# The group norm of a two-block transformer's first attention: its inverse root as a power on GpSimd

## The chip, the cores and the metric

The kernel runs on one core of a Trainium2 chip. The metric is the device time of one execution in microseconds, as the median of several runs. Engines are called TensorE (PE in the rows), VectorE (DVE), ScalarE (ACT), GpSimd (POOL) and SyncE (SP); PEld is TensorE's load of weights.

## What is computed

Two transformer blocks of depth 1 over 1024 tokens of width 1024, in float32. The first block has an RMS norm, a projection, four differential heads (two softmaxes each, subtracted) and eight heads with forget gates, an output projection and a gated feed-forward part. The second has two causal convolutions, eight heads of stick-breaking attention and a feed-forward part with a squared ReLU. The change touches only the norm of the differential heads' outputs:

```python
def rmsnorm(x, g):
    xf = x.astype(jnp.float32)
    y = xf * lax.rsqrt(jnp.mean(xf * xf, axis=-1, keepdims=True) + EPS)
    return (y * g.astype(jnp.float32)).astype(x.dtype)
...
            p = (jax.nn.softmax(jnp.where(chunk_mask, s1, NEG), axis=-1)
                 - lam * jax.nn.softmax(jnp.where(chunk_mask, s2, NEG), axis=-1))
            od = jnp.einsum('bhqk,bhkd->bhqd', p.astype(dv_t.dtype), dv_t)
...
        od_b = rmsnorm(od_b, subln_g[l]) * (1.0 - lam_init)
```

It is taken over the 128 values of a head, for each of four heads and 1024 tokens, with EPS = 1e-5.

## The kernel before

Activations lie transposed in SBUF: 128 features on the partitions, tokens along the row, in two halves of 512. A float32 product of a weight tile is made of three matmuls of 128x512: weights rounded to a high part (`wh`, written by ScalarE, L2411) and a rest (`lows`, written by GpSimd, L2655), each with the activations' high part (L1801, L1803), and `wh` with their rest (L1806). ScalarE and GpSimd make these parts for each piece of weights ahead of TensorE; there are seven buffers for values and rests and four for high parts.

In the stage around the change, attention of one head and the projection of the next ones are interleaved: between score blocks (L1879, L1880), transposes (L1893) and products with the values (L1911, L1914) TensorE takes pieces of projection. VectorE takes a score block's maximum (`max`, L2077 and L2079), ScalarE its exponential with the sum (L2508), VectorE divides (L2096 to L2104). It also evacuates the projections: `qkv_evac` (L2057, L2059) into a stage buffer, and `rotate` (L2066). GpSimd finishes the rotation (L2661, L2679) and splits q and k (L2692, L2694).

A head's output is gathered in four groups of 256 tokens in `mix`, a single buffer of 128x1024 (`diff_out`, L2142; in the later heads with forget gates `pair_out`, L2148). After the last group the norm follows, in two halves of 512 tokens:

- `sub_square`: ScalarE squares `mix` into a stage buffer `i` (L2534).
- `sub_sum`: TensorE multiplies by a matrix of ones, so that each row of PSUM holds the sum over the head (L1921).
- `sub_norm` on VectorE: `va` = -(mean + EPS) / 2 into a stage buffer `j` (L2155).
- `sub_roots`, once for both halves, on ScalarE: y = exp(-0.5 ln(-2 va)), two logarithms (L2540), then two exponentials (L2544). The compiler puts a table load before each pair.
- `sub_norm` on GpSimd, for each half: y (1.5 + va y y), a Newton step, times the gain, and the product into `mix` (L2701, L2703, L2706, L2708, L2710), each waiting for the one before by a semaphore.

The signal `sub` of the last operation frees both stage buffers of its half and lets SyncE spill `mix` to DRAM (L2816); the next write into `mix` waits for that spill. The first writer after the heads one to three is L2142, after the fourth L2148.

The order of work on each engine is not written by hand. `work_order` lays the steps out; `engine_orders` counts each step with rough costs (`about`), lays all engines' steps out on a time axis (`lay_out`), ranks the steps of all engines but TensorE by how late they may run, and repeats that three times; the best result is each engine's order. So a changed cost or step can move others on every engine.

Of the kernel before, what the change touches and what calls it, by code (L numbers as in the profile page):

```python
# [10 lines left out]
ALU = mybir.AluOpType  # L11
ACT = mybir.ActivationFunctionType
# [52 lines left out]
class Part:  # L65


    def __init__(self, place, step):
        self.place, self.step, self.needs, self.gives, self.takes, self.shared, self.bytes = place, step, [], [], 0.0, 0.0, 0
        self.rank = self.start = self.end = 0.0  # L70


def elements(ap):
    n = 1
    for d in ap.shape[1:]:
        n *= d
    return n


def about(engine, op, a, k):  # L80

    n = elements(a[0])
    if engine == "sync":
        return 350.0
    if engine == "tensor":
        if op == "transpose":
            return 110.0
        n = elements(a[2])
        if a[2].dtype == F:
            return max(4 * n / 2.4, 150.0)  # L90
        return 127.0 if a[2].dtype == BF else max((n + 32) / 2.4, 110.0)
    if engine == "scalar":
        return 205 + 0.833 * n
    if engine == "gpsimd":
        if op == "dma_start":
            return 900.0
        return 150 + (1.2 if op == "tensor_scalar" else 2.4) * n
    if op == "tensor_tensor_reduce":
        return 160 + 1.04 * n
    if op == "reduce_max":  # L100
        return 160 + 1.04 * elements(a[1])
    if op == "tensor_tensor_scan":
        return 160 + 2.08 * n
    if n <= 8:
        return 160.0
    if op == "memset" or op == "tensor_scalar" and in_sbuf(op, a):
        return 120 + 0.52 * n
    return 160 + 1.04 * n


def in_sbuf(op, a):

    return op != "memset" and all("PS" not in str(x) for x in a[:4])


class Uncounted:


# [3 lines left out]
    def __getattr__(self, op):  # L122
        def call(*a, **k):
            if self.sg is not None and op != "wait_ge":
                if self.sg.log is not None and op != "then_inc":
                    self.sg.log.takes += about(self.engine, op, a, k)
                    if self.engine == "vector" and in_sbuf(op, a) and elements(a[0]) > 8:
                        self.sg.log.shared += about(self.engine, op, a, k)
                    if op == "dma_start":
                        self.sg.log.bytes += 4 * 128 * elements(a[0])  # L130
            return self
        return call
# [677 lines left out]
class Attention:  # L810
# [60 lines left out]
    def group_steps(self, g, u, a, c, jobs, slot, last):  # L871
        O = self.O
        pending = None
        first = [True]

        def pv(kp, x, end=False):
            given = []
            if first[0]:
                given = O.claim(self.OB) + u.v
            O.step("pv", u=u, a=a, c=c, g=g, kp=kp, x=x, first=first[0], given=given, ob=self.OB)  # L880
            first[0] = False
            self.pt_given[x] = [("pv", (g, kp))]
            u.pv_done = ("pv", (g, kp))

        for kp in range(c + 1):
            tb, given = O.next_t()
            x = self.turned % 2
            self.turned += 1
            O.step("turn", u=u, g=g, kp=kp, c=c, slot=slot, p=[("p", j["key"]) for j in jobs], tb=tb, given=given, x=x, pt=list(self.pt_given[x]))
            if kp == c:  # L890
                self.p_given[slot] = [("turned", (g, kp))]
            O.bank_given[tb] = [("pt_hi", (g, kp)), ("pt_lo", (g, kp))]
            if pending is not None:
                pv(*pending)
            pending = (kp, x)
            yield
        pv(*pending)
        qc = slice(256 * c, 256 * c + 256)
        done = ("pv", (g, c))
        out = ("mix", (g, "out"))  # L900
        if u.kind == DIFF:
            O.step("diff_out", g=g, c=c, qc=qc, done=done, ob=self.OB, given=list(self.mix_given))
            O.bank_given[self.OB] = [out]
        else:
            i, gi = O.next_stage()
            O.step("pair_out", g=g, a=a, qc=qc, done=done, ob=self.OB, i=i, gi=gi, given=list(self.mix_given))
            O.bank_given[self.OB] = [("pair_lo", g), out]
            O.stage_given[i] = [out]
        if not last:
            return  # L910
        row = u.index + (0 if u.kind == DIFF else 4)
        if u.kind == DIFF:
            yield
            squares, roots = [], []
            for half in range(2):
                i, gi = O.next_stage()
                O.step("sub_square", g=g, half=half, i=i, gi=gi, out=out)
                squares.append(i)
            means = [O.next_stage() for _ in range(2)]
            for half in range(2):  # L920
                i = squares[half]
                yield
                b = self.OB
                O.step("sub_sum", g=g, half=half, i=i, b=b, given=O.claim(b))
                yield
                j, gj = means[half]
                O.step("sub_norm", g=g, half=half, i=i, j=j, gj=gj, b=b)
                roots.append((half, i, j))
                if half:
                    O.step("sub_roots", g=g, roots=roots)  # L930
                O.bank_given[b] = [("sub_mean", (g, half))]
                out = ("sub", (g, half))
                O.stage_given[i] = [out]
                O.stage_given[j] = [out]
                yield
        if self.direct is None:
            O.step("spill_mix", row=row, out=out, key=(self.name, row))
            self.mix_given = [("spilled", (self.name, row))]
            self.spills[row] = ("spilled", (self.name, row))
            return  # L940
        dst, ready, free = self.direct
        self.mix_given = []
        for half in range(2):
            key = (self.name, row, half)
            O.step("mix_split", dst=dst, row=row, half=half, key=key, out=out, given=[free])
            ready[row] += [("row_hi", key), ("row_lo", key)]
            self.mix_given += [("row_hi", key), ("row_lo", key)]
        self.spills[row] = None
# [983 lines left out]
def vector_program(e, w, sg, T, steps):  # L1932
    PS = T.PS
    stage, sm, rstd = T.stage, T.sm, T.rstd
    for s in steps:
        kind = s["kind"]
# [9 lines left out]
        elif kind == "lambda":  # L1946
            w.wait_ge(*sg.at("vec", 0))
            e.tensor_tensor(T.gfa, T.vec[:, V_GF:V_GF + 8], T.vec[:, V_GA:V_GA + 8], ALU.mult).then_inc(*sg.up("gfa", 0))
            e.tensor_tensor(sm[:, 2:4], T.vec[:, V_LAM:V_LAM + 2], T.vec[:, V_LAM + 2:V_LAM + 4], ALU.mult)
            e.tensor_scalar(sm[:, 1:2], T.v(V_SUB), 1.0 - LAM_INIT, None, ALU.mult).then_inc(*sg.up("lam_steps", "in"))  # L1950
        elif kind == "lambda_out":
            w.wait_ge(*sg.at("lam_exp", 0))
# [9 lines left out]
        elif kind == "h_in":  # L1962
            k, half = s["e"], s["half"]
# [12 lines left out]
        elif kind == "end_square" and s["i"] is not None:  # L1976
            k, half = s["e"], s["half"]
# [423 lines left out]
def scalar_program(e, w, sg, T, steps):  # L2401
    PS, stage, sm = T.PS, T.stage, T.sm
    for s in steps:
# [127 lines left out]
        elif kind == "sub_square":  # L2531
            for event in s["gi"] + [s["out"]]:
                w.wait_ge(*sg.at(*event))
            e.activation(stage[s["i"]], T.mix[:, cols(s["half"])], ACT.Square).then_inc(*sg.up("sub_sq", (s["g"], s["half"])))  # L2534
        elif kind == "sub_roots":
            for half, i, j in s["roots"]:
                key = (s["g"], half)
                w.wait_ge(*sg.at("sub_mean", key))
                w.wait_ge(*sg.at("sub_summed", key))
                e.activation(stage[i], stage[j], ACT.Ln, scale=-2.0).then_inc(*sg.up("sub_ln", key))  # L2540
            for half, i, j in s["roots"]:
                key = (s["g"], half)
                w.wait_ge(*sg.at("sub_ln", key))
                e.activation(stage[i], stage[i], ACT.Exp, scale=-0.5).then_inc(*sg.up("sub_root", key))  # L2544
        elif kind == "mix_split" or kind == "row_split":
            half, row = s["half"], s["row"]
            if kind == "mix_split":
# [97 lines left out]
def gpsimd_program(e, w, sg, T, steps):  # L2645
    stage = T.stage
    for s in steps:
# [48 lines left out]
        elif kind == "sub_norm":  # L2696
            key, half = (s["g"], s["half"]), s["half"]
            y, va = stage[s["i"]], stage[s["j"]]
            m = T.mix[:, cols(half)]
            w.wait_ge(*sg.at("sub_root", key))  # L2700
            e.tensor_tensor(va, va, y, ALU.mult).then_inc(*sg.up("sub_part", (key, 0)))  # L2701
            w.wait_ge(*sg.at("sub_part", (key, 0)))
            e.tensor_tensor(va, va, y, ALU.mult).then_inc(*sg.up("sub_part", (key, 1)))  # L2703
# [192 lines left out]
def lay_out(lanes, ahead):  # L2896


    given, free, moved = {}, {engine: 0.0 for engine in lanes}, 0.0
    laid = []  # L2900
    at = {(engine, kind): 0 for engine in lanes for kind in lanes[engine]}
    left = sum(len(parts) for kinds in lanes.values() for parts in kinds.values())
    while left:
# [28 lines left out]
                        start, kind, part = begin, other, urgent  # L2932
        part.start = start
        end = start + part.takes
        if engine == "vector" and free["gpsimd"] > start:
            end += 0.6 * min(part.shared, free["gpsimd"] - start)
        free[engine] = end
# [163 lines left out]
```

## Time and profile before

| | us |
|---|---|
| median of 3 runs | 2393.03 (2392.59 to 2394.03) |
| the profiled execution, its own time | 2393.43 |
| its span, first to last instruction | 2391.6 |
| TensorE's matmuls busy | 2339.2 |
| VectorE, GpSimd, ScalarE busy | 1892.4, 1117.8, 1089.0 |

The span is what the trace covers; the execution's own time holds 1.8 us around it. Busy time of an engine doesn't say that it bounds the kernel: where matmuls are busy all the time, what other engines do is hidden. The granted clock is TensorE's, as a share of 2.4 GHz.

### The profile page before, as it was taken

The page shows a single profiled execution, that of the slowest core. Times are in us where ns is not written, and L with a number is a line of the kernel's source. Part 1 is how long each engine was busy: PE and PEld are TensorE (multiplying, and loading weights), DVE is VectorE, ACT ScalarE, POOL GpSimd, SP SyncE. Part 2 cuts the span into 40 slices and gives each one's busy share as a digit, 9 for nine tenths or more (in the row PEclk, how much of TensorE's full clock was granted, in tenths as well). Part 3 has the DMA queues.
Part 4 walks back from the last instruction along what each step waited for, and adds up shares of the span by engine and source line. Part 5 has one row for each costly group of instructions (what it writes and reads, how often), then busy time and mean ns, then how long its engine had stood idle before and what let it go on. Part 6 is the DMA issues. An engine that isn't in the chain of part 4 may idle for free.

```text
span 2391.6 us, 31516 instructions
## 1 busy us (share of the span) xinstructions
PE 2339.2 (98%) x11126; PEld 1933.7 (81%) x11126; DVE 1892.4 (79%) x2593; ACT 1089.0 (46%) x1867; POOL 1117.8 (47%) x786
## 2 busy tenths in 40 slices
PE   9999999999999999999999999999999999999998
PEld 7777778878788888888887877887878888888886
DVE  6777759784687998899967956778288889999986
ACT  6455556562543333353444436555163333544433
POOL 4766652221534664445543553431154466455553
PEclk9999999999999999999999999999999999999999
DMA  4312321242122333264513862223223444754522
GB/s 159 80 45 58 89 76 58 79 129 77 47 74 84 104 104 111 88 210 123 183 58 116 185 153 63 62 60 106 82 82 113 150 150 164 239 160 151 179 89 106
DMA packets 228763, 265.83 MB, mean 111 GB/s; under 512 B 18296, under 2 KB 139640, under 8 KB 228480
## 3 DMA queue, kind: packets, MB, share of 16 engines
q1 hardware_dynamic: 225008, 251.50, 33.5%
q0 software_dynamic: 3168, 11.54, 2.6%
q8 instruction: 90, 1.47, 0.3%
q10 hardware_dynamic: 432, 0.79, 0.1%
q14 instruction: 65, 0.53, 0.1%
HBM read 173.02 MB, written 60.33 MB: 98 GB/s over the span
## 4 chain that ended last, share of the span: by engine, by line
PE 84%; DVE 6%; POOL 3%; ACT 3%; issue 2%; DMA 1%; SPq 0%; POOLq 0%; DVEq 0%; ACTq 0%
PE PS L1801 24%; PE PS L1806 24%; PE PS L1803 24%; PE PS L1893 3%; PE PS L1914 2%; PE PS L1911 2%; PE PS L1879 2%; PE PS L1880 1%; DVE R L2242 1%; ACT R L2565 1%; POOL stage L2679 0%; DVE X L2173 0%; DVE Pb L2102 0%; DVE X L2290 0%; DVE Pb L2104 0%
## 5 line engine op out<-in xcount | busy, mean ns | idle before, releaser
L1801 PE MATMUL PS<-R,wh 128*128 128x512 f32 x2872 | 1138.7, 396 | 9.9 <-DVE stage L2066 2.8
L1806 PE MATMUL PS<-R,wh 128*128 128x512 f32 x2872 | 1122.3, 391 | 3.6 <-DVE R L2238 2.0
L2655 POOL TENSOR_TENSOR lows<-values,wh 128x512 fp32r<-128x512 f32 (+1 forms) x486 | 689.4, 1423 | 899.2 <-ACT wh L2411 737.3
L1803 PE MATMUL PS<-R,lows 128*128 128x512 f32 x2564 | 1001.4, 391 | 0.5 <-POOL lows L2655 0.5
L1801 PEld LDWEIGHTS PS<-R,wh 128*128 128x128 f32 x2872 | 540.4, 188 | 123.7 <-DVE stage L2066 4.5
L1806 PEld LDWEIGHTS PS<-R,wh 128*128 128x128 f32 x2872 | 539.8, 188 | 122.7 <-DVE R L2238 3.7
L2411 ACT ACTIVATE wh<-values 128x512 fp32r<-128x512 f32 (+2 forms) x487 | 301.9, 620 | 613.1 <-PE PS L1806 608.8
L1803 PEld LDWEIGHTS PS<-R,lows 128*128 128x128 f32 x2564 | 482.8, 188 | 95.6 <-issue 4.1
L2290 DVE TENSOR_TENSOR X<-PS,X 128x1024 f32<-128x1024 f32 x154 | 187.2, 1216 | 23.1 <-PE PS L1806 22.5
L2655 POOL TENSOR_TENSOR late_r<-late,wh 128x512 fp32r<-128x512 f32 x77 | 107.8, 1400 | 125.1 <-DVE values L2187 54.7
L2525 ACT ACTIVATE PT<-PS 128x512 fp32r<-128x512 f32 (+1 forms) x200 | 109.0, 553 | 111.0 <-PE PS L1893 89.1
L1803 PE MATMUL PS<-R,late_r 128*128 128x512 f32 x308 | 119.9, 389 | 0.0
L1879 PE MATMUL PS<-R 128*128 128x512 f32 (+2 forms) x288 | 105.2, 369 | 12.2 <-ACT P L2508 7.2
L1893 PE MATMUL PS<-ident,Pb 128*128 128x128 f32 x720 | 107.3, 273 | 8.4 <-DVE PT L2135 3.1
L2114 DVE TENSOR_TENSOR_SCAN Pb<-TABF,steps 128x128 f32<-128x128 f32 (+3 forms) x64 | 94.6, 1486 | 20.4 <-ACT TABF L2517 12.3
L1893 PEld LDWEIGHTS PS<-ident,Pb 128*128 128x128 f32 x720 | 84.6, 141 | 27.4 <-issue 8.5
L2279 DVE TENSOR_TENSOR R1f<-R1f 128x512 f32<-128x512 f32 x88 | 95.3, 1112 | 13.1 <-ACT R1f L2610 12.2
L2193 DVE TENSOR_TENSOR stage<-PS,stage 128x512 f32<-128x512 f32 x140 | 94.4, 681 | 12.1 <-PE PS L1806 10.4
L1880 PE MATMUL PS<-R 128*128 128x512 f32 (+2 forms) x288 | 97.3, 348 | 0.0
L1911 PE MATMUL PS<-PT,R 128*128 128x256 f32 x480 | 89.6, 282 | 3.4 <-issue 1.8
L2411 ACT ACTIVATE wh<-late 128x512 fp32r<-128x512 f32 x77 | 48.5, 629 | 95.5 <-PE PS L1806 95.5
L2137 DVE TENSOR_TENSOR PT<-PS,PT 128x512 fp32r<-128x512 f32 (+1 forms) x120 | 75.0, 632 | 20.7 <-ACT PT L2525 19.7
(278 smaller groups left out, 2976.5 us busy)
## 6 DMA issues: line engine op xcount, KB each, us to landing
scr_hid<-R1f SPq DMA_DIRECT2D x160, 256.0 KB, 2.7
values<-w_in_dram SPq DMA_DIRECT2D x88, 256.0 KB, 2.9
R1f<-scr_hid SPq DMA_DIRECT2D x88, 256.0 KB, 3.8
R0f<-scr_hid SPq DMA_DIRECT2D x86, 256.0 KB, 3.7
values<-w_ff_dram SPq DMA_DIRECT2D x60, 256.0 KB, 3.0
values<-w_ff_dram SPq DMA_DIRECT2D x100, 128.0 KB, 2.5
R<-R SPq DMA_DIRECT2D x96, 128.0 KB, 2.3
X<-X POOLq DMA_DIRECT2D x22, 512.0 KB, 5.7
```

Of the source, the lines that this page charges most:

```text
L1801: e.matmul(PS[:, b, :], wh, high, start=s["start"], stop=False, skip_group_check=on)
L1803: e.matmul(PS[:, b, :], wl, high, start=False, stop=False, skip_group_check=on)
L1806: m = e.matmul(PS[:, b, :], wh, low, start=False, stop=s["stop"], skip_group_check=on)
L1879: e.matmul(S2[:, k0:k1], q, u.KH[:, a, k0:k1], start=True, stop=False)
L1880: m = e.matmul(S2[:, k0:k1], q, u.KL[:, a, k0:k1], start=False, stop=True)
L1893: m = e.transpose(PS[:, s["tb"], at:at + 128], T.Pb[:, s["slot"], par, 128 * kt:128 * kt + 128], T.ident[:, :])
L1911: e.matmul(o, lhs, T.PT[:, x, 0, kk], start=s["first"] and n == 0, stop=False)
L2279: e.tensor_tensor(T.hid_sum(a), one, other, op).then_inc(*sg.up("block", ("sum", *key)))
L2290: e.tensor_tensor(x, T.PS[:, s["b"]:s["b"] + 2, :], x, ALU.add).then_inc(*sg.up("block", s["key"]))
L2411: e.activation(T.wh[:, piece.h, 0:m], T.wv[piece.v][:, 0:m], ACT.Copy).then_inc(*sg.up("w_hi", piece.n))
L2525: e.activation(T.PT[:, s["x"], 0, 0:m], PS[:, s["tb"], 0:m], ACT.Copy, bias=bias).then_inc(*sg.up("pt_hi", key))
L2655: e.tensor_tensor(T.wl[piece.v][:, 0:m], T.wv[piece.v][:, 0:m], T.wh[:, piece.h, 0:m].bitcast(F), ALU.subtract).then_inc(*sg.up("w_lo", pi ...
```

## The change

`sub_roots` and its four activations per head are gone. In their place GpSimd takes -2 va, and that to the power of -0.5, as an operation on two tensors whose second input is one column, broadcast; the column is written once by VectorE. The Newton step stays. GpSimd now waits for `sub_mean` and no more for `sub_root`.

The planner gets a rule: an activation whose function isn't the one of the last table counts 1283 ns more on ScalarE.

```diff
+TABLES = (ACT.Exp, ACT.Ln, ACT.Sqrt, ACT.Silu, ACT.Sigmoid)
+TABLE_LOAD = 1283.0
...
+                    if op == "activation" and a[2] in TABLES:
+                        self.sg.log.tables.append(a[2])
...
-                roots.append((half, i, j))
-                if half:
-                    O.step("sub_roots", g=g, roots=roots)
...
+            e.memset(sm[:, 116:117], -0.5)
...
-        elif kind == "sub_roots":
-            for half, i, j in s["roots"]:
-                key = (s["g"], half)
-                w.wait_ge(*sg.at("sub_mean", key))
-                w.wait_ge(*sg.at("sub_summed", key))
-                e.activation(stage[i], stage[j], ACT.Ln, scale=-2.0).then_inc(*sg.up("sub_ln", key))
-            for half, i, j in s["roots"]:
-                key = (s["g"], half)
-                w.wait_ge(*sg.at("sub_ln", key))
-                e.activation(stage[i], stage[i], ACT.Exp, scale=-0.5).then_inc(*sg.up("sub_root", key))
...
-            w.wait_ge(*sg.at("sub_root", key))
+            w.wait_ge(*sg.at("sub_mean", key))
+            e.tensor_scalar(y, va, -2.0, None, ALU.mult).then_inc(*sg.up("sub_part", (key, "mean")))
+            w.wait_ge(*sg.at("sub_part", (key, "mean")))
+            w.wait_ge(*sg.at("lam_steps", "in"))
+            e.tensor_tensor(y, y, T.sm[:, 116:117].broadcast_to([128, 512]), ALU.pow).then_inc(*sg.up("sub_part", (key, "root")))
+            w.wait_ge(*sg.at("sub_part", (key, "root")))
             e.tensor_tensor(va, va, y, ALU.mult).then_inc(*sg.up("sub_part", (key, 0)))
...
+        for function in part.tables:
+            if function != table:
+                table, end = function, end + TABLE_LOAD
```

In the changed file the lines of TensorE, VectorE and ScalarE have numbers higher by five (L2066 is L2071 there, L2137 is L2142, L2142 is L2147, L2411 is L2416, L2508 is L2513), those of GpSimd ahead of the norm lower by five (L2655 is L2650); the new operations are L2696 and L2699, and L2701 to L2710 keep their numbers.

ScalarE at the norm of the first head, before. `mix` is the head's output, `stage` the buffers:

```order
L2534 ACTIVATE stage<-mix 128x512 [waits s_mix]
L2534 ACTIVATE stage<-mix 128x512 [waits s_qk_lo,s_qk_hi]
L2508 ACTIVATE P_61,sm<-PS,sm 128x384 [waits s_max,s_p]
L2411 ACTIVATE wh<-values 128x512 [waits s_dense,s_raw6]
L2508 ACTIVATE Pb,sm<-PS,sm 128x512 [waits s_max]
L2540 ACT_TABLE_LOAD [waits s_sub_summed]
L2540 ACTIVATE stage<-stage 128x512 [waits s_sub_mean]
L2540 ACTIVATE stage<-stage 128x512 [waits s_sub_summed,s_sub_mean]
L2544 ACT_TABLE_LOAD
L2544 ACTIVATE stage<-stage 128x512 [waits s_sub_ln] x2
L2411 ACTIVATE wh<-values 128x512 [waits s_dense,s_raw0]
L2508 ACTIVATE P_61,sm<-PS,sm 128x512 [waits s_max,s_p]
```

And with the change:

```order
L2539 ACTIVATE stage<-mix 128x512 [waits s_mix]
L2539 ACTIVATE stage<-mix 128x512 [waits s_qk_lo,s_qk_hi]
L2530 ACTIVATE PT<-PS 128x384 [waits s_pv,s_turned]
L2416 ACTIVATE wh<-values 128x512 [waits s_dense,s_raw6]
L2513 ACTIVATE Pb,sm<-PS,sm 128x512 [waits s_max]
L2416 ACTIVATE wh<-values 128x512 [waits s_dense,s_raw0]
L2513 ACTIVATE P_61,sm<-PS,sm 128x512 [waits s_max,s_p]
```

The loads, logarithms and exponentials are gone, the weight split follows the score block's exponential at once, and one exponential (L2508 before, L2513 now) has moved ahead of the squares.

GpSimd at the same place, with the change. The first row is the weight split's neighbour, a rotation; the last two follow the norm's second half:

```order
L2656 TENSOR_TENSOR stage<-stage,TABF 128x512 [waits s_permuted]
L2696 TENSOR_SCALAR stage<-stage 128x512 [waits s_sub_mean]
L2699 TENSOR_TENSOR stage<-stage,sm 128x512 [waits s_lam_steps,s_sub_part]
L2701 TENSOR_TENSOR stage<-stage 128x512 [waits s_sub_part]
L2703 TENSOR_TENSOR stage<-stage 128x512 [waits s_sub_part]
...
L2710 TENSOR_TENSOR mix<-mix,stage 128x512 [waits s_sub_part]
L2674 TENSOR_TENSOR stage<-stage 128x512 [waits s_rot_sin,s_rot_cos]
L2650 TENSOR_TENSOR lows<-values,wh 128x512 [waits s_w_hi]
```

Two operations stand ahead of the five of each half; a rotation and a weight split stand behind the norm, as before.

VectorE behind the norm, before:

```order
L2104 TENSOR_SCALAR Pb<-Pb,sm 128x640 [waits s_inverse]
L2137 TENSOR_TENSOR PT<-PS,PT 128x512 [waits s_pt_hi]
L2077 MEMSET PS 64x64 [waits s_scores]
L2079 TENSOR_REDUCE sm<-PS 128x1 [waits s_masked]
L2066 TENSOR_TENSOR stage<-PS,TABF 128x512 [waits s_permuted,s_sub]
L2096 RECIPROCAL sm<-sm 128x1 [waits s_exp]
```

And with the change:

```order
L2082 MEMSET PS 64x64 [waits s_scores]
L2084 TENSOR_REDUCE sm<-PS 128x1 [waits s_masked]
L2071 TENSOR_TENSOR stage<-PS,TABF 128x512 [waits s_permuted,s_sub]
L2082 MEMSET PS 64x64 [waits s_scores]
L2084 TENSOR_REDUCE sm<-PS 128x1 [waits s_masked]
L2142 TENSOR_TENSOR PT<-PS,PT 128x512 [waits s_pt_hi]
```

The rotation that waits for the norm's first half (`s_sub`) now stands ahead of one more maximum and of the evacuation of a transpose. TensorE's own order differs in exchanges of neighbouring steps up to about 600 us and around the second attention, and is the same in the feed-forward stages; apart from the norm every engine issues the same matmuls, activations and transfers; one table load of the second attention (L2637) is gone too.

## Rows read from the trace of the kernel before

**Rows 1.** The page: span, busy time, chain that ended last.

```profile
span 2391.6 us, 31516 instructions
...
PE 2339.2 (98%) x11126; PEld 1933.7 (81%) x11126; DVE 1892.4 (79%) x2593; ACT 1089.0 (46%) x1867; POOL 1117.8 (47%) x786
...
PE 84%; DVE 6%; POOL 3%; ACT 3%; issue 2%; DMA 1%; SPq 0%; POOLq 0%; DVEq 0%; ACTq 0%
```

**Rows 2.** Table by stretches: busy time by engine, granted clock, DMA share, GB/s.

```profile
0.00:350.00 350.00, 329.43 (x1647) 265.11 (x1648) 253.59 (x492) 191.60 (x350) 211.78 (x161) 1.00 0.29 84
...
2350.00:2391.60 41.60, 32.22 (x158) 27.01 (x156) 27.21 (x48) 13.70 (x23) 11.46 (x9) 0.86 0.33 120
```

**Rows 3.** Waits of TensorE, 120 to 350 us: total, times, longest.

```profile
PE PS L1879 <- ACT P L2508: 6.2, 3, 2.5
...
PE PS L1801 <- DVE late L2059: 1.4, 1, 1.4
```

**Rows 4.** Timeline, first head's norm: start, us, instructions, [idle before].

```profile
136.15 1.28 ACT L2540 ACT_TABLE_LOAD   x1
...
139.91 1.15 ACT L2544 ACTIVATE stage<-stage 128x512 f32<-128x512 f32 x2
...
142.39 0.47 PE L1879 MATMUL PS<-R 128*128 128x512 f32 x1 [2.51 <-ACT P L2508]
```

**Rows 5.** Chain of work by time, first and fourth head: start, us.

```profile
140.62 1.27 POOL stage L2701
...
174.15 1.73 POOL lows L2655
...
335.07 1.30 POOL late L2701
...
346.70 1.29 POOL mix L2710
```

**Rows 6.** Groups of ScalarE's instructions: busy us, mean ns, idle before.

```profile
L2540 ACT ACT_TABLE_LOAD x4 | 5.1, 1283 | 0.1
```

**Rows 7.** Groups of GpSimd's instructions at the norm.

```profile
L2701 POOL TENSOR_TENSOR stage<-stage 128x512 f32<-128x512 f32 x6 | 8.6, 1427 | 9.9 <-ACT stage L2544 9.9
...
L2706 POOL TENSOR_SCALAR stage<-stage,sm 128x512 f32<-128x512 f32 x7 | 5.7, 815 | 0.7
...
L2701 POOL TENSOR_TENSOR late<-late,stage 128x512 f32<-128x512 f32 x1 | 1.3, 1288 | 1.8 <-ACT stage L2544 1.8
```

**Rows 8.** Timeline of GpSimd, first and second head.

```profile
140.62 1.27 POOL L2701 TENSOR_TENSOR stage<-stage 128x512 f32<-128x512 f32 x1 [4.60 <-ACT stage L2544]
141.97 1.27 POOL L2703 TENSOR_TENSOR stage<-stage 128x512 f32<-128x512 f32 x1
...
204.82 1.29 POOL L2701 TENSOR_TENSOR stage<-stage 128x512 f32<-128x512 f32 x1 [2.41 <-ACT stage L2544]
...
214.17 0.69 POOL L2706 TENSOR_SCALAR stage<-stage,sm 128x512 f32<-128x512 f32 x1
...
216.32 1.42 POOL L2710 TENSOR_TENSOR mix<-mix,stage 128x512 f32<-128x512 f32 x1
```

**Rows 9.** Timeline of VectorE: first, second, third and fourth head.

```profile
136.00 0.69 DVE L2155 TENSOR_SCALAR stage<-PS 128x512 f32<-128x512 f32 x1 [0.67 <-PE PS L1921]
...
219.91 0.68 DVE L2057 SCALAR_TENSOR_TENSOR stage<-PS,rstd 128x512 f32<-128x512 f32 x1
...
289.83 0.42 DVE L2142 COPY mix<-PS 128x256 f32<-128x256 f32 x1
...
348.02 0.69 DVE L2059 TENSOR_TENSOR late<-PS,rstd 128x512 f32<-128x512 f32 x1 [1.89 <-POOL mix L2710]
...
352.40 0.42 DVE L2148 TENSOR_TENSOR mix<-PS,stage 64x256 f32<-64x256 f32 x1 [2.64 <-DMA scr_mix<-mix]
```

**Rows 10.** SyncE's spill of mix: third head's issue, landing of all.

```profile
285.04 0.33 SPq L2816 DMA_DIRECT2D scr_mix<-mix  x1
...
DMA to landing us min/median/max: 2.6/2.6/4.5
```

More of the change, by code:

```diff
@@ L70, in __init__ @@
         self.rank = self.start = self.end = 0.0
+        self.tables = []
 def elements(ap):
@@ L913, in group_steps @@
             yield
-            squares, roots = [], []
+            squares = []
             for half in range(2):
@@ L2899, in lay_out @@
     given, free, moved = {}, {engine: 0.0 for engine in lanes}, 0.0
-    laid = []
+    laid, table = [], None
     at = {(engine, kind): 0 for engine in lanes for kind in lanes[engine]}
```

## The prediction

> **What bounds the kernel now.** The page comes first: TensorE's matmuls are busy for 98% of the span, and of the chain of work that ended last 84% is TensorE, 3% GpSimd and 3% ScalarE [rows 1]. So an edit counts where TensorE stands idle, or where it makes it so. The table by stretches says where: in the first 350 us, the stage in which the first attention's four differential heads run, matmuls are busy for 329.4 us and idle for 20.6, of 52.4 in the whole span [rows 1, 2]. The waits of TensorE from 120 to 350 us, where all four group norms lie, name ScalarE's exponential at L2508 first, with 6.2 us in three waits; the others are for VectorE, such as 1.4 us for its L2059 [rows 3]. Nothing there names GpSimd.
>
> ScalarE's timeline at the first head shows where those waits come from. A table load, two logarithms, a second load and two exponentials hold it from 136.15 to 141.06 us, with a weight split and then the exponential of a score block behind them; the matmuls at L1879 stood idle for 2.51 us until that exponential had read its banks [rows 4].
>
> The chain of work by time shows a second thing. In the first head it leaves ScalarE at 140.6 us and stays on GpSimd: the ten operations of the norm, then the rotation, the splits of q and k and a weight split, up to 175.9 us. In the fourth head it also runs over all ten, from 335.07 to 347.99 us, and leaves through VectorE's L2059 [rows 5, 9]. There the reader is to see that GpSimd, 47% busy on the mean, has no room just behind the norm. In heads two and three the chain goes through ScalarE's block instead.
>
> **What is removed.** Per head two table loads of 1283 ns, two logarithms and two exponentials of about 0.62 us: with their overlaps 4.9 us of ScalarE, four times [rows 4, 6]. On TensorE this is worth what it waited for: 6.2 us at most [rows 3]. I take all of it. GpSimd's wait for the second exponential goes too. The first product (L2701) waited 4.60 us in head one, and 11.7 us over the four heads (9.9 and 1.8) [rows 7, 8]. GpSimd was free then, so each norm starts earlier by that: 4.6 and 2.4 us in the first two heads [rows 8], the 2.9 left of the 9.9 in the third and 1.8 in the fourth [rows 7]. The means that the new code needs are ready by then: the second ends at 136.69 us in head one [rows 9], and the first of the pair is all that the first half wants.
>
> **What is added.** Eight times (four heads, two halves) GpSimd gets a multiplication by -2 and a power, in line with the five operations that stand there. The multiplication is one operation on one input; the nearest row is L2706, two operations on one input, 0.815 us in the mean [rows 7]. With the gaps of some 0.1 us that a wait for its own semaphore leaves between two operations [rows 8], a half costs 1.0 us plus the power, P. A head costs 2P + 2.0.
>
> No row shows a power on GpSimd. From below it is bounded by the product of two inputs, 1.29 us for 128x512 [rows 8]: it reads as much and computes more. From above I take each of some 40 elementary operations (a logarithm and an exponential as polynomials with guards) at the price of a whole product: 52 us. Inside one instruction operands needn't be read and written each time, so the nearest row is again L2706: two operations for 0.69 us at its fastest, its start included [rows 8], at most 0.35 each. Some 25 operations (my count, an estimate) then make **P = 8.6 us**. I take that.
>
> The Trainium skill's GPSIMD Engine Reference (3.1, Elementwise) says that a loop of up to two operations per element is bound by its ports, and a longer one by about three operations a cycle at 1.2 GHz. By that page my 25 operations come to an estimated 3.6 us, and the sum below to +14 us, 2408 us; no row here has a loop long enough to show it.
>
> **Who waits.** GpSimd's queue is in order, so weight splits, rotations and the splits of the next head's q and k stand behind the power. VectorE waits for the norm in two ways: L2066, L2057 and L2059 want the stage buffers that it frees, and the copy into mix (L2142; after head four L2148) wants the spill of mix, which lands 2.6 us after its issue [rows 9, 10]. VectorE runs in order too: behind such a wait stand the maxima and the evacuations that TensorE needs. Room before it stalls: in head one none, since the chain itself runs over GpSimd; in head two 2.2 us (the norm ends at 217.74, L2057 starts at 219.91); in head three the spill, issued at 285.04, lands at 287.64 and its copy starts at 289.83, again 2.2; in head four none, since VectorE already waited 1.89 us for the norm and 2.64 us for the spill [rows 8 to 10]. That such a wait reaches TensorE is shown there: it waited 1.4 us for that L2059 [rows 3]. SyncE's queue has the splits' small transfers and the weight loads behind the spill; the loads are issued pieces ahead, and I add nothing for them.
>
> **The sum**, as 2P + 2.0 less the earlier start and the room: 2P - 2.6, 2P - 2.6, 2P - 3.1 and 2P + 0.2, together 8P - 8.1 us. With P = 8.6 that is 60.7 us; less the 6.2 us of waits for ScalarE it is +54.5. I pass delays of over ten microseconds a head to TensorE in full. The memset of one column and the new wait for lam_steps, long given, cost nothing: the start of VectorE's program covers both, and without cover it would be some 0.1 us.
>
> The planner's new rule, 1283 ns per change of table, moves steps on all engines up to the second attention. TensorE's order differs in small exchanges within the first 600 us and around 1400 to 1700 us, and is the same in the feed-forward stages. I put 0 on it, and 5 us to either side as an estimate: a quarter of the 20.6 us that TensorE is idle in the first stage [rows 2].
>
> The profiled execution took 2393.43 us, its span is 2391.6 [rows 1], and the median of three runs is 2393.03: 0.4 us apart, so the sum stands against either. **Forecast: 2448 us.**
>
> **Rivals.** (1) *The power is as cheap as a product*, P = 1.29. The operation is one instruction of the same shape on the same engine, and GpSimd has idle time ahead of each norm. The first three heads then lose nothing, the fourth 2.8 us, and the 6.2 us are gained: -3.4 us, **2390**, to 2385 with a lucky order. This is the case on the other side; it decides below P = 1.8, where 8P - 8.1 equals 6.2. Against it: two operations that only multiply and add already take 0.69 us. (2) *The power runs apart from all these rows*, above 52 us, as a loop that isn't pipelined would. Each head then holds GpSimd for over 100 us, longer than the 64 us from one norm to the next [rows 8], VectorE stands at the copy into mix, and TensorE stands with it: more than 8 x 52 - 8.1 - 6.2, **above 2795**. TensorE would then be idle for tens of microseconds; in the last stretch, where it is idle for a quarter of the time, its granted clock was 0.86 of 2.4 GHz [rows 2], so some matmuls after each stall could run slower. The same page (3.2, Cross-partition) has a GpSimd reduction of 128x2048 at 247,699 ns, 121 ns per element; a power at that rate would be an estimated 62 us and the sum +482, 2875 us. No run here shows such an operation. (3) *TensorE absorbs it*: with P near 3 a head adds about 3 us, which banks and pieces made ahead may hide; the time is then **2403 or less**, down to no change. For it speaks that TensorE has never waited long for GpSimd [rows 3]; against it the chain in rows 5. (4) *The planner's exchanges are the whole effect*, within 5 us; that needs P below 2 as well, and is counted with (1).
>
> **How the numbers follow.** What a measurement of this kernel can tell from no change is about 0.2%, 4.8 us. The main case, P between 2 and 52, has 0.58, of which 0.08 is (3); rival (1) with (4) has 0.25, half of it past -4.8 us by the planner's luck and half within; rival (2) has 0.17. So faster 0.13, same 0.13, slower 0.74. The range starts at 2385, which takes in rival (1) whole, and ends at 2795, where P is 52; only rival (2) is left out. Within it the main case alone spans 2395 to 2795.
>
> **What would show it.** In the changed profile, the mean of the new TENSOR_TENSOR at L2699 is P. I expect the norm's eight table loads gone; no TensorE wait for L2508 behind one; GpSimd's line for the norm about 8 x (8.6 + 0.9) = 76 us longer; a VectorE wait for L2710 or for the spill in every head, of 10 to 17 us; and TensorE's busy time unchanged at 2339 us, with idle time grown by what the span grew. I am wrong in size if P isn't near 8.6, and wrong in mechanism if P is large and VectorE doesn't wait, or if the time grows by other than about 8P.

## The result, and the profile after

The changed kernel takes **3038.15 us** (four runs, 3036.41 to 3039.31) against 2393.41 us before: a ratio of 1.2688, 95% interval 1.2673 to 1.2702. The forecast of 2448 us and its range up to 2795 us missed it by far.

The page of the changed kernel, its span, busy times, the slices of TensorE, GpSimd and the granted clock, and the chain that ended last; it answers to [rows 1]:

```profile
span 3037.4 us, 31486 instructions
...
PE 2358.5 (78%) x11126; PEld 1951.2 (64%) x11126; DVE 1880.5 (62%) x2594; ACT 1070.7 (35%) x1842; POOL 1784.3 (59%) x802
...
PE   9801600701700999999999999999999999999998
...
POOL 5599799799799331434655554353432435645553
PEclk9955855855855999999999999999999999999999
...
PE 68%; POOL 25%; DVE 5%; issue 1%; ACT 1%; DMA 0%; SPq 0%; POOLq 0%; DVEq 0%; ACTq 0%
```

Each slice is 76 us. The four holes in TensorE's line are the four heads. There GpSimd is busy nearly all the time and the granted clock falls to between 0.5 and 0.6; behind the thirteenth slice TensorE is busy at the full clock again, nearly as before. GpSimd's share of the chain rose from 3% to 25%. ScalarE is 18.3 us less busy, 10.3 of it for eight table loads.

GpSimd's timeline in the first head (start, duration, what, idle before) answers to [rows 8]:

```profile
137.10 1.50 POOL L2696 TENSOR_SCALAR stage<-stage 128x512 f32<-128x512 f32 x1 [0.39 <-DVE stage L2160]
138.69 81.96 POOL L2699 TENSOR_TENSOR stage<-stage,sm 128x512 f32<-128x512 f32 x1
220.73 1.26 POOL L2701 TENSOR_TENSOR stage<-stage 128x512 f32<-128x512 f32 x1
...
228.37 81.95 POOL L2699 TENSOR_TENSOR stage<-stage,sm 128x512 f32<-128x512 f32 x1
...
315.23 1.26 POOL L2710 TENSOR_TENSOR mix<-mix,stage 128x512 f32<-128x512 f32 x1
```

**One power takes 81.96 us**, 64 times the 1.27 us of a product of the same shape. VectorE's and TensorE's waits, with their total, number and longest:

```profile
DVE stage L2062 <- POOL mix L2710: 239.6, 3, 81.1
DVE stage L2071 <- POOL mix L2710: 161.3, 2, 81.1
DVE late L2064 <- POOL mix L2710: 157.2, 1, 157.2
...
DVE stage L2064 <- POOL mix L2710: 78.5, 1, 78.5
```

```profile
PE PS L1805 <- DVE stage L2071: 161.1, 2, 80.6
PE PS L1863 <- DVE stage L2062: 159.2, 2, 79.8
PE PS L1805 <- DVE late L2064: 156.6, 1, 156.6
PE PS L1897 <- DVE Pb L2107: 80.9, 2, 79.9
PE PS L1915 <- DVE mix L2147: 77.2, 1, 77.2
```

VectorE waited 636.6 us for the norm's last product (L2710), which frees the stage buffers; TensorE waited 635.0 us for what stood behind in VectorE's queue. The eight powers take 655.7 us, so nearly all of it came through. The chain of delays is the one forecast. In the first three heads VectorE waits twice, once for each half, and in the fourth once for both.

### The profile page after: what moved, and what is told of

It reads as the page before. It is cut to its first block, busy times and chain, and to the rows that moved or that the text cites. A ratio compares the mean times of both kernels' runs of the same rounds, so it can differ in the third digit from the quotient of the medians.

```text
span 3037.4 us, 31486 instructions
## 1 busy us (share of the span) xinstructions
PE 2358.5 (78%) x11126; PEld 1951.2 (64%) x11126; DVE 1880.5 (62%) x2594; ACT 1070.7 (35%) x1842; POOL 1784.3 (59%) x802
## 4 chain that ended last, share of the span: by engine, by line
PE 68%; POOL 25%; DVE 5%; issue 1%; ACT 1%; DMA 0%; SPq 0%; POOLq 0%; DVEq 0%; ACTq 0%
PE PS L1805 20%; PE PS L1810 20%; PE PS L1807 20%; POOL stage L2699 19%; POOL late L2699 3%; PE PS L1897 2%; PE PS L1915 1%; PE PS L1918 1%; PE PS L1883 1%; PE PS L1884 1%; DVE R L2247 1%; PE PS L1863 0%; POOL stage L2696 0%; DVE X L2295 0%; ACT R L2560 0%
## 5 line engine op out<-in xcount | busy, mean ns | idle before, releaser
L2650 POOL TENSOR_TENSOR lows<-values,wh 128x512 fp32r<-128x512 f32 (+1 forms) x486 | 692.3, 1430 | 879.9 <-ACT wh L2416 723.6
L2699 POOL TENSOR_TENSOR stage<-stage,sm 128x512 f32<-128x512 f32 x7 | 573.8, 81974 | 0.6
L2416 ACT ACTIVATE wh<-values 128x512 fp32r<-128x512 f32 (+2 forms) x487 | 302.0, 620 | 633.1 <-PE PS L1810 629.6
L2650 POOL TENSOR_TENSOR late_r<-late,wh 128x512 fp32r<-128x512 f32 x77 | 109.1, 1417 | 123.6 <-ACT wh L2416 56.1
L1897 PE MATMUL PS<-ident,Pb 128*128 128x128 f32 x720 | 109.3, 278 | 84.5 <-DVE Pb L2107 80.9
L2062 DVE SCALAR_TENSOR_TENSOR stage<-PS,rstd 128x512 f32<-128x512 f32 x24 | 16.4, 686 | 254.1 <-POOL mix L2710 239.6
L2496 ACT ACTIVATE R<-stage 64x512 fp32r<-64x512 f32 x45 | 28.2, 628 | 356.3 <-POOL stage L2674 183.6
L1863 PE MATMUL PS<-stage,perm 128*128 128x512 f32 x32 | 19.9, 722 | 159.3 <-DVE stage L2062 159.2
L1915 PEld LDWEIGHTS PS<-PT,R 128*128 128x128 f32 x480 | 80.2, 193 | 91.5 <-DVE mix L2147 77.6
L1883 PE MATMUL PS<-R 128*128 128x512 f32 (+2 forms) x288 | 108.0, 378 | 10.4 <-ACT P L2513 4.3
L1863 PEld LDWEIGHTS PS<-stage,perm 128*128 128x128 f32 x32 | 6.5, 221 | 163.4 <-DVE stage L2062 159.8
```

The lines of the kernel that those rows point to most:

```text
L1883: e.matmul(S2[:, k0:k1], q, u.KH[:, a, k0:k1], start=True, stop=False)
L1897: m = e.transpose(PS[:, s["tb"], at:at + 128], T.Pb[:, s["slot"], par, 128 * kt:128 * kt + 128], T.ident[:, :])
L1915: e.matmul(o, lhs, T.PT[:, x, 0, kk], start=s["first"] and n == 0, stop=False)
L2416: e.activation(T.wh[:, piece.h, 0:m], T.wv[piece.v][:, 0:m], ACT.Copy).then_inc(*sg.up("w_hi", piece.n))
L2650: e.tensor_tensor(T.wl[piece.v][:, 0:m], T.wv[piece.v][:, 0:m], T.wh[:, piece.h, 0:m].bitcast(F), ALU.subtract).then_inc(*sg.up("w_lo", pi ...
L2699: e.tensor_tensor(y, y, T.sm[:, 116:117].broadcast_to([128, 512]), ALU.pow).then_inc(*sg.up("sub_part", (key, "root")))
```

## The experiments

The diffs of this part are shown without their semaphore calls.

**How long a power is.** Three kernels shorten it; the planner is told 512 columns, and the columns left out keep -2 va. The traces show every engine's instructions in the order of the changed kernel, in these three, in the two kernels after them and in the one of "The room below".

```diff
-e.tensor_tensor(y, y, T.sm[:, 116:117].broadcast_to([128, 512]), ALU.pow)
+e.tensor_tensor(y[:, 0:52], y[:, 0:52], T.sm[:, 116:117].broadcast_to([128, 52]), ALU.pow)
```

> The power is taken over 52 of 512 columns (the other columns of y stay -2 va, so the norm is wrong there); orders as in the changed kernel. If its length goes by columns, 0.16 us each, P is 8.3 to 8.6 us, the size that the prediction took. Theory A: 8 x 8.4 - 14.3 = +53, 2446 us. Rival C (banks and pieces made ahead absorb short holds): below 2425 us. Rival D (a power's length is mostly fixed, or goes by something else than columns): P far from 8.4, and the time still 8P - 14.3 above before.

> The power is taken over 256 of 512 columns (the rest of y stays -2 va); orders as in the changed kernel. P about 41 us by columns. Theory A: 8 x 41 - 14.3 = +314, 2707 us. Rival E (TensorE's clock falls in long waits and each return costs extra, so that the time grows faster than 8P): more than 2715 us here, if the 3 us that the full power took over the sum are such a cost it is within 3 us of A.

> The power over 12 of 512 columns (wrong elsewhere), orders as in the changed kernel. By 0.34 + 0.159 us per column P = 2.25 us, 1.2 us more than the product that stood there in the run called mult (2392.9). Theory A, whose slope of 8 held from 1.0 to 82 us: 8 x 1.2 = 10 us over mult, 2403 us. Rival C (short holds are absorbed, the slope sets in above some microseconds): 2393 to 2397 us.

A fourth takes all columns of 32 partitions:

```diff
+e.tensor_tensor(y[0:32, :], y[0:32, :], T.sm[0:32, 116:117].broadcast_to([32, 512]), ALU.pow)
```

> The power over 32 of 128 partitions, all 512 columns (wrong elsewhere). If the length goes by columns alone, 82 us and 3038 us in all, as in the changed kernel. If it goes by elements, about 21 us, and 8 x 21 - 8.8 = 159 us more than before, 2552 us.

And one has a product in the power's place:

```diff
+e.tensor_tensor(y, y, T.sm[:, 116:117].broadcast_to([128, 512]), ALU.mult)
```

> The power is a product instead (y times -0.5, so the norm's values are not the reference's); every engine's order is that of the changed kernel. Theory A (the power's own length is the whole loss, P per operation, time = before + 8P - 14.3 us where each head's term is positive): with P = 1.3 heads one to three lose nothing, so 2390 us, -3.4, between 2385 and 2395. Rival B (the planner's new orders, or GpSimd's place in the chain, cost much by themselves): 2400 us or more even without a power.

The groups of that instruction (total, mean ns, idle before), in the changed kernel, with 256, 52 and 12 columns, with 32 partitions, and with the product:

```profile
L2699 POOL TENSOR_TENSOR stage<-stage,sm 128x512 f32<-128x512 f32 x7 | 573.8, 81974 | 0.6
```

```profile
L2701 POOL TENSOR_TENSOR stage<-stage,sm 128x256 f32<-128x256 f32 x7 | 288.2, 41171 | 0.6
```

```profile
L2701 POOL TENSOR_TENSOR stage<-stage,sm 128x52 f32<-128x52 f32 x7 | 60.8, 8689 | 0.6
```

```profile
L2701 POOL TENSOR_TENSOR stage<-stage,sm 128x12 f32<-128x12 f32 x7 | 16.2, 2320 | 0.6
```

```profile
L2699 POOL TENSOR_TENSOR stage<-stage,sm 32x512 f32<-32x512 f32 x7 | 573.7, 81963 | 0.6
```

```profile
L2699 POOL TENSOR_TENSOR stage<-stage,sm 128x512 f32<-128x512 f32 x7 | 7.5, 1065 | 0.6
```

The length goes by columns: (81.97 - 41.17) / 256 = 0.159 us each, and a start of about 0.4. Partitions don't count: 32 take as long as 128. Now the sum of the prediction can be tested. One term has to be mended first: the multiplication by -2 took 1.52 us in the mean, not 0.815, which adds 8 x 0.7 = 5.6 us. The sum is then 8P - 8.7. It was mended after these runs; as recorded, 8P - 14.3, it gives +55.2 us with 52 columns, 7 us too few.

| kernel | P, us | 8P - 8.7 | measured: median, less the one before on the same chip | ratio (interval) |
|---|---|---|---|---|
| product | 1.07 | -0.1 | 2392.92 - 2393.55 = -0.6 | 0.9996 (0.9987 to 1.0005) |
| 12 columns | 2.32 | +9.9 | 2401.42 - 2394.42 = +7.0 | 1.0030 (1.0019 to 1.0041) |
| 52 columns | 8.69 | +60.8 | 2456.09 - 2393.55 = +62.5 | 1.0260 (1.0246 to 1.0274) |
| 256 columns | 41.17 | +320.7 | 2711.92 - 2393.55 = +318.4 | 1.1332 (1.1317 to 1.1348) |
| all, 32 partitions | 81.96 | +647.0 | 3034.38 - 2394.42 = +640.0, one run | |
| the change | 81.97 | +647.1 | 3038.15 - 2393.41 = +644.7 | 1.2688 (1.2673 to 1.2702) |

Over a range of 1 to 82 us the time follows the length with a slope near 8, one for each power: from row to row, without the one of 32 partitions, it is 6.1, 8.7, 7.9 and 8.0. The first of these is the change of 7.6 us over 1.25 us of P; with some 3 us of uncertainty it doesn't fix a slope. So theory A holds for the length. Rival C falls: with 12 columns, where a hold is only 2.3 us, the time is 7 us above before (4.5 to 9.8), not within 4 us. Rival D falls, since 52 columns took the length that columns give, and so does rival B of the product's kernel: with a cheap operation the new orders don't make it 2400 us or more. Rival E falls as well: from 41 to 82 us the slope is (3038.15 - 2711.92) / 40.8 = 8.0, so the slower clock in and behind the waits costs nothing that grows with them.

**The room below.** The multiplication in the form of L2706, on top of the product (the wait for `lam_steps` moves ahead of it):

```diff
-e.tensor_scalar(y, va, -2.0, None, ALU.mult)
+e.tensor_scalar(y, va, 0.0, T.sm[:, 116:117], ALU.add, ALU.mult)
```

> Mult, with the one-operation TENSOR_SCALAR at L2696 (1.49 to 1.6 us) written in the form of L2706, an addition and a product with a column of sm (0.69 us there); values wrong as in mult, by another factor too. If the form sets the length, it takes about 0.7 us; if writing to another buffer than is read does, it stays at 1.5 us. Theory A: with 0.7 us, up to 6 us less than mult, 2387 us. Rival C: the same time as mult, since nothing waits there.

Here is the product's kernel, and then this one:

```profile
L2696 POOL TENSOR_SCALAR stage<-stage 128x512 f32<-128x512 f32 x6 | 9.7, 1610 | 23.0 <-DVE stage L2160 23.0
```

```profile
L2697 POOL TENSOR_SCALAR stage<-stage,sm 128x512 f32<-128x512 f32 x6 | 5.0, 836 | 22.4 <-DVE stage L2160 22.4
```

The form sets the length, not the other buffer: 0.84 us with two operations, 1.61 with one. Whether it is the second operation or the column of `sm` in the constant's place wasn't tried apart. The time is 2389.67 against 2394.42 before, 0.9977 (0.9968 to 0.9986), and 4.1 us below the product's -0.6, of the 6.2 that eight times 0.77 would be. The effect is there; its slope, 5.3, is too uncertain to tell from 8 with intervals of 2 us to either side.

**The planner's rule.** It was put on the kernel before, and taken out of the change and of the product's kernel:

```diff
         for function in part.tables:
             if function != table:
-                table, end = function, end + TABLE_LOAD
+                table = function
```

That is how it is taken out; the kernel before got the lines of the change that belong to it.

> The kernel before, with logarithms and exponentials on ScalarE, laid out with the rule of 1283 ns per change of table. Theory A: within 5 us of 2393. Rival B: the rule moves the time by more than 5 us, and its sign then stands in the change too.

> The change without the planner's rule, the full power. Theory A (the power is the loss, the orders worth a few us): 3035 us, between 3030 and 3045. Rival B (the new orders put the waiting steps of VectorE behind the norm, and the old ones would let it run on): under 3000 us.

> A product in place of the power (wrong values), and the rule of 1283 ns per change of table out of the planner. The rule alone cost 3.3 us on the kernel before, where a new order lets TensorE wait 2.8 us near 93 us and its clock falls. Theory A (that cost comes with the rule whatever stands at the norm, and ScalarE's freed 4.9 us a head are a gain of their own): 3 us under the run with the rule, 2390 us or a little less. Rival F (the gain of 3 us is not there, the two runs' difference is chance of the layout): 2392 to 2396 us.

| kernel | with the rule | without |
|---|---|---|
| as before | 2396.84, 1.0012 (1.0004 to 1.0021) | 1 |
| the change | 3038.15, 1.2688 (1.2673 to 1.2702) | 3032.83, 1.2666 (1.2649 to 1.2683) |
| the product | 2392.92, 0.9996 (0.9987 to 1.0005) | 2387.85, 0.9972 (0.9961 to 0.9983) |

The rule costs 0.12% on the kernel before (3.3 us) and 0.24% on the product (5.7 us, where 3 were expected); with the full power, where the intervals overlap, the difference, 5.3 us by ratios, has the same sign. Rival F falls, and so do both rivals B: alone the rule moves the time by less than 5 us, and the old orders with the full power don't come under 3000 us. At one place the traces show a part of it. With the rule TensorE waits near 93 us, in the kernel before the change with the rule:

```profile
93.62 0.77 PE L1886 MATMUL PS<-R 128*128 128x512 f32 x1 [2.61 <-ACT P L2515]
```

and its table by stretches of 5 us (matmuls busy, loads, VectorE, ScalarE, GpSimd, clock, DMA share, GB/s):

```profile
90.00:95.00 5.00, 2.39 (x13) 2.04 (x12) 4.74 (x13) 2.44 (x6) 2.81 (x2) 0.78 0.36 102
95.00:100.00 5.00, 5.00 (x18) 4.21 (x17) 3.73 (x8) 2.55 (x6) 1.27 (x1) 0.53 0.01 2
```

Without it the same stretch of the kernel before reads:

```profile
90.00:95.00 5.00, 4.06 (x19) 2.54 (x18) 4.86 (x12) 2.38 (x6) 4.81 (x4) 1.00 0.40 107
```

So a wait of 2.6 us and some 5 us near half the clock come with the rule. TensorE's idle time from 0 to 100 us is 6.0 us with the rule and 4.2 without. That a new order causes the wait is read from the two traces; no run changed this place alone, and what else of the rule's cost sits in the later stages wasn't taken apart.

**A power where it costs little.** After the sum by a matrix of ones all 128 partitions hold the same 512 means, so 127 of 128 values are raised for nothing. As the length goes by columns and not by partitions, one value per token can be laid as 128x8. The kernel leaves out two more things: VectorE writes mean + EPS itself, so no multiplication by -2 is needed, and the Newton step is gone. GpSimd has two operations for each half in place of seven. Cut to its core:

```diff
+        elif kind == "root_out":
+            e.dma_start(T.scr_root[s["row"]:s["row"] + 1, cols(s["half"])], stage[s["j"]][0:1, :])
+        elif kind == "root_in":
+            e.dma_start(T.rt[:, 0:8], T.scr_root[s["row"]].rearrange("(p c) -> p c", c=8))
...
+        elif kind == "root":
+            e.tensor_tensor(T.rt[:, 8:16], T.rt[:, 0:8], T.sm[:, 116:117].broadcast_to([128, 8]), ALU.pow)
...
+        elif kind == "root_back":
+            e.dma_start(T.scr_root[4 + s["row"]].rearrange("(p c) -> p c", c=8), T.rt[:, 8:16])
+        elif kind == "root_fan":
+            e.dma_start(stage[s["j"]], T.scr_root[r:r + 1, cols(s["half"])].broadcast_to([128, 512]))
...
+            e.tensor_scalar(va, va, 0.0, T.sm[:, 1:2], ALU.add, ALU.mult)
             e.tensor_tensor(m, m, va, ALU.mult)
```

> The power over 8 columns instead of 512: every partition holds the same means, so row 0 of each half goes to DRAM, comes back as 128x8 (one value per token), is raised, goes to DRAM and comes back as a row for every partition; the Newton step is left out, GpSimd only multiplies by the gain and into mix. Four transfers one after another, 2.6 us each by the spill's landing, take the place of the root: 136.7 + 4 x 2.6 + 1.6 + 4.2 = 153 us for the first head, as before (153.97). Theory A (only the time for which GpSimd is held counts): no loss from the power, 8 x 4.6 us less on GpSimd, ScalarE free: 2385 to 2392 us. Rival G (SyncE's queue in order: weight loads stand behind the waits for the means and for the root, and TensorE starves; or the chain of transfers is longer than 10 us and mix comes free late): 2400 us or more.

> The same without the planner's rule. Theory A: 3 us under the run with the rule. Rival G: 2400 us or more, by the same waits.

With the planner's rule it takes 2394.43 us, 0.9997 (0.9988 to 1.0005). Without it **2387.08 us, 0.9969 (0.9958 to 0.9979): faster than both kernels**, by 0.3% or 7.4 us under the one before. In the first head of that one VectorE has the second half's means ready at 137.83 us, and GpSimd goes on:

```profile
137.14 0.69 DVE L2172 TENSOR_SCALAR stage<-PS 128x512 f32<-128x512 f32 x1 [0.60 <-PE PS L1937]
```

```profile
142.98 1.66 POOL L2706 TENSOR_TENSOR rt<-rt,sm 128x8 f32<-128x8 f32 x1
144.63 1.28 POOL L2662 TENSOR_TENSOR lows<-values,wh 128x512 fp32r<-128x512 f32 x1
145.87 1.29 POOL L2668 TENSOR_TENSOR stage<-stage,TABF 128x512 f32<-128x512 f32 x1
149.68 0.70 POOL L2713 TENSOR_SCALAR stage<-stage,sm 128x512 f32<-128x512 f32 x1 [2.52 <-DMA stage<-scr_root]
...
153.07 1.29 POOL L2715 TENSOR_TENSOR mix<-mix,stage 128x512 f32<-128x512 f32 x1
```

The root is back in all partitions at 149.68 us, 11.85 after the means, by its length nearly four landings and the power (12.1), though part of it is GpSimd, which finishes a split at 142.90 before it takes the power. Mix is done at 154.36, as in the kernel before (153.97). But GpSimd splits and rotates in between, and ScalarE has only the squares left of the norm. Rival G, 2400 us or more, falls. The kernel with the rule is 6.7 us by ratios above the other, between theory A's 2392 us and the rival's 2400. The rule is all that differs between the two; where its order loses the time wasn't taken apart.

This is the table's line for 100 to 350 us in the kernel before, and, without the rule, with the product and with the short power:

```profile
100.00:350.00 250.00, 233.66 (x1202) 189.14 (x1201) 188.69 (x384) 136.23 (x261) 153.27 (x114) 1.00 0.24 67
```

```profile
100.00:350.00 250.00, 241.61 (x1247) 196.06 (x1247) 193.31 (x396) 119.67 (x244) 177.45 (x132) 0.99 0.24 68
```

```profile
100.00:350.00 250.00, 243.68 (x1272) 198.90 (x1271) 192.54 (x403) 120.23 (x247) 131.11 (x98) 1.00 0.28 79
```

With the short power ten of the 16.3 us of TensorE's idle time in this stretch are gone, with the product eight. The two kernels' ratios, 0.9969 and 0.9972 (0.9961 to 0.9983), aren't told apart, although GpSimd is 46 us less busy with the short power. So what is gained over the kernel before comes most likely from ScalarE's freed block, which both have, and not from GpSimd's; in the first head of the short kernel GpSimd waits 2.52 us for the last transfer, so there the transfers set the norm's end.

## Why the prediction was wrong

- **The price of the power** is the step that failed. The prediction made 8.6 us of some 25 operations at 0.35 us, half of a two-operation row; it is 81.97. The product was no near row for it, and the upper bound, 40 operations at the price of a whole product, 52 us, was none either. Counting the operations of a function bounds nothing while neither their number nor their rate is in a row. The estimate by the rule of the Trainium skill's GPSIMD Engine Reference (3.1, Elementwise), 3.6 us, was further off still. The rate of the reduction on the same page of the Trainium skill (3.2, Cross-partition), worked out as an estimated 121 ns per element, was the nearest of all, against 159 ns per column here, and stood in the rival of 0.17; no run here has that reduction. The range should have gone on to it.
- **Where the delay goes** was right: in order through GpSimd, then VectorE, then TensorE, in full. With the measured P the sum 8P - 14.3 gives +641.5, against +644.7. The slope is shown; that the whole comes within 3 us is in part luck. The sum put the planner's rule at 0. Without the rule the measured loss is 3032.83 - 2394.53 = 638.3 us where the mended sum has 647.1, and the product's kernel is 6.7 us under before where it has -0.1. So the sum's other terms are 7 to 9 us too high, and the rule's cost of 5 to 6 us hid most of that. Which of them is too high (a room, a start, the waits for ScalarE) stays open.
- **Which wait ends last** was half right. The stage buffers (L2062, L2064, L2071) hold VectorE for 636.6 us. None of VectorE's waits in the changed kernel is put down to the spill of mix. In the first head the norm ends at 316.49 us and the copy into mix (L2147) starts at 322.05, more than the 2.6 us of a landing later. And in the first three heads the wait comes once for each half, where the prediction had one for each head.
- **A reading of the chain**: it doesn't stay on GpSimd all the way to 175.9 us in the first head. From 155.96 to 157.25 us it passes over two copies on ScalarE (L2491, L2492). Nothing in the sum hangs on that.
- **The multiplication** was mis-sized, 1.52 us for 0.815, +5.6 us. The row taken as the nearest had two operations, and one takes longer. The lower bound was off too: the product in the power's form took 1.07 us, not 1.29.
- **ScalarE's 6.2 us**: with the product TensorE's waits for that exponential between 120 and 350 us fell from 6.2 [rows 3] to 1.3 us:

```profile
PE PS L1883 <- ACT P L2513: 1.3, 3, 0.8
```

  So most of them were there to be had. The product's kernel is only 0.6 us under the one before with the planner's rule and 6.7 without: the rule, put at 0, took the gain back.
- **The planner** at 0, give or take 5 us: it costs 3 to 7 us, in one direction. That is nearly the whole gain of the small case, and under 1% of the loss in the large one.
- **Rival (2)** was the case that came: TensorE idle for tens of microseconds, the clock near half. Its further cost, matmuls slowed after each stall, doesn't show: TensorE's busy time, forecast unchanged, grew by 19.3 us, yet the time doesn't grow by more than the powers' length. That TensorE would otherwise have waited in these 19.3 us fits, but isn't shown apart.
- **Rival (1)** didn't come, as P isn't a product's. What it said of a cheap root, -3.4 us, was tried with the product: -0.6 us (-3.1 to +1.2) with the rule, -6.7 without. **Rival (3)**, that TensorE absorbs short holds, didn't come either; 12 columns, a hold of 2.3 us, gave +7.0 us of the sum's 9.9, so little or nothing is absorbed there.

## What to carry to other kernels

A function that no row of the trace shows has a price that must be measured before it goes into an in-order queue with other work; eight calls of it cost 27% here. What is computed alike on all partitions should be asked for its shape first: one value per token as 128x8 took 1.66 us where 128x512 twice took 164, for the price of transfers there and back. And a better cost in a planner that ranks by its own forecast may make worse orders: change one thing at a time.

## What was not expected of the hardware

- GpSimd's power takes 0.159 us per column, whatever the number of partitions (81.96 us for 32 and 81.97 for 128). Whether it depends on the values, and what VectorE would take for the same power, wasn't tried.
- GpSimd's TENSOR_SCALAR with one multiplication by a constant takes 1.5 to 1.6 us for 128x512 in the mean of a group; with an addition and a multiplication by a column it takes 0.69 to 0.85, and 0.95 in the kernel with the short power and the rule.
- A product with its second input one broadcast column took 1.07 us, less than the 1.29 to 1.46 us of the groups with two full inputs in the same kernel.
- The time grows by 8.0 us for each microsecond of the power's length, from 41 to 82 us, and from the product to the full power by 645.3 us where 8 x 80.9 is 647.2: no cost of TensorE's long waits beyond what they last shows. TensorE's granted clock in the first head's two waits was near the lower of its two levels, 1.2 GHz, as the table by stretches of the changed kernel shows behind GpSimd's busy time:

```profile
133.00:223.00 90.00, 12.87 (x61) 9.48 (x59) 8.98 (x21) 7.05 (x16) 86.94 (x5) 0.60 0.02 6
223.00:313.00 90.00, 9.84 (x35) 7.70 (x35) 5.40 (x12) 1.48 (x3) 89.49 (x8) 0.56 0.00 0
```
